# Paged attention: value pages issued from ScalarE, probabilities copied out ahead of the next maximum

## The reference

```python
def latent_attention(q_lat, q_rope, k_lat, k_rope, q_pos, k_pos):
    s = (jnp.einsum('bqhc,bkc->bhqk', ql, k_lat).astype(jnp.float32)
         + jnp.einsum('bqhr,bkr->bhqk', qr, k_rope).astype(jnp.float32)) * scale
    s = jnp.where(k_pos[None, :] <= qp[:, None], s, NEG_INF)
    p = jax.nn.softmax(s, axis=-1).astype(k_lat.dtype)
    return jnp.einsum('bhqk,bkc->bqhc', p, k_lat)
...
past = [(cache_ckv[j][page_table].reshape(bs, n_pages * PAGE_SIZE, MLA_KV_LORA),
         cache_krope[j][page_table].reshape(bs, n_pages * PAGE_SIZE, MLA_D_ROPE))
```

## Time and profile before

| | |
|---|---|
| median of 3 runs | 4748.0 us (4743.9 to 4748.29) |
| profiled execution | 4758.49 us, span 4756.7 us |
| TensorE busy | 4029.0 us, 85% |
| VectorE busy | 3155.6 us, 66% |
| ScalarE busy | 1374.6 us, 29% |
| GpSimd busy | 1164.6 us, 24% |
| mean granted TensorE clock | 0.931 |
| paged attention | from about 2728 us to 2995 us |

### The profile page before, as it was taken

One profiled execution on the slowest core, in us unless ns is written; L12 is line 12 of the kernel. 1 busy time (PEld: TensorE's weight loads), 2 busy tenths in 40 slices (PEclk: granted clock), 3 DMA queues, 4 the chain that ended last, 5 costly groups with the idle time before them and its releaser, 6 DMA issues.

```text
span 4756.7 us, 60298 instructions
## 1 busy us (share of the span) xinstructions
PE 4029.0 (85%) x19517; PEld 3147.9 (66%) x19517; DVE 3155.6 (66%) x6719; ACT 1374.6 (29%) x2253; POOL 1164.6 (24%) x1217
## 2 busy tenths in 40 slices
PE   8999678857999999999488868889569999999994
PEld 1454334456999999999346512344469999999994
DVE  0134556996878878878545512558977887887886
ACT  0120013366333333333112100123573333333331
POOL 0000011275323323323100000002672332333332
PEclk9998689989999999999779978899799999999997
DMA  9777675445888888887377666744458888888883
GB/s 317 248 259 248 230 244 196 158 171 221 293 288 284 292 285 285 291 287 259 142 241 228 195 185 198 233 163 161 173 220 270 284 292 285 285 291 287 284 288 118
DMA packets 494570, 1151.15 MB, mean 242 GB/s; under 512 B 45310, under 2 KB 268559, under 8 KB 491104
## 3 DMA queue, kind: packets, MB, share of 16 engines
q1 hardware_dynamic: 293330, 689.92, 42.9%
q0 software_dynamic: 95824, 350.11, 22.5%
q10 hardware_dynamic: 105296, 109.71, 6.7%
HBM read 952.47 MB, written 197.09 MB: 242 GB/s over the span
## 4 chain that ended last, share of the span: by engine, by line
PE 53%; DVE 19%; DMA 9%; ACT 7%; issue 6%; SPq 3%; POOL 2%; POOLq 1%; ACTq 0%; DVEq 0%
PE ps L1550 16%; PE ps L1531 12%; PE ps L1547 6%; PE ps L272 4%; DMA arena<-in_peer_uT 4%; PE ps L440 3%; ACT u_parts_d L1584 3%; DMA x<-in_peer_uT 3%; DVE v_parts_d L1688 2%; PE ps L251 2%; DVE u_parts_d L1684 2%; DVE arena L1722 2%; DVE x L1705 1%; ACT arena L1449 1%; DVE a_parts_d L1697 1%
## 5 line engine op out<-in xcount | busy, mean ns | idle before, releaser
L1531 PE MATMUL ps<-h_parts_d,u_parts_d 128*128 128x384 f32 x6144 | 1114.5, 337 | 114.1 <-DVE u_parts_d L1684 70.8
L1531 PEld LDWEIGHTS ps<-h_parts_d,u_parts_d 128*128 128x128 f32 x6144 | 1066.2, 188 | 153.3 <-ACT arena L1591 99.2
L1550 PE MATMUL ps<-a_parts_d,v_parts_d 128*128 128x384 f32 x4608 | 809.0, 334 | 0.0
L1550 PEld LDWEIGHTS ps<-a_parts_d,v_parts_d 128*128 128x128 f32 x4608 | 799.6, 188 | 0.0
L272 PE MATMUL ps<-ring,hT 128*128 128x512 f32 (+1 forms) x1440 | 645.5, 607 | 24.4 <-DMA ring<-in_gla_wo 13.7
L1586 ACT ACTIVATE v_parts_d<-ring 128x1024 fp32r<-128x1024 f32 x256 | 250.1, 1048 | 940.3 <-PE ps L1550 940.3
L272 PEld LDWEIGHTS ps<-ring,hT 128*128 128x128 f32 (+1 forms) x1440 | 253.4, 179 | 392.0 <-issue 387.7
L1684 DVE TENSOR_TENSOR u_parts_d<-ring,u_parts_d 128x1024 fp32r<-128x1024 f32 x256 | 313.5, 1225 | 198.0 <-ACT u_parts_d L1584 197.4
L1653 POOL DMA_INDIRECT arena<-in_peer_v,arena x256 | 243.3, 950 | 815.4 <-DVE ps L1722 806.7
L1653 POOL DMA_INDIRECT hT<-u_rows,arena x256 | 291.8, 1140 | 373.0 <-DVE hT L1705 329.2
L1722 DVE SCALAR_TENSOR_TENSOR ps<-arena,ps 128x1024 f32<-128x1024 f32 x256 | 329.3, 1286 | 16.2 <-DVE arena L1712 11.3
(11 more groups left out here) (277 smaller groups left out, 4487.9 us busy)
## 6 DMA issues: line engine op xcount, KB each, us to landing
ring<-in_peer_uT SPq DMA_DIRECT2D x256, 512.0 KB, 5.9
ring<-in_peer_v SPq DMA_DIRECT2D x256, 512.0 KB, 7.3
arena<-in_peer_uT SPq DMA_DIRECT2D x186, 512.0 KB, 5.5
u_rows<-arena SPq DMA_DIRECT2D x440, 128.0 KB, 4.0
ring<-in_ada_w SPq DMA_DIRECT2D x96, 512.0 KB, 4.6
gates_dense<-arena ACTq DMA_DIRECT2D x24, 2048.0 KB, 6.3
x<-gates_dense ACTq DMA_DIRECT2D x64, 768.0 KB, 7.8
u_rows<-arena SPq DMA_DIRECT2D x76, 512.0 KB, 6.0
```

Source lines behind the costliest of these rows:

```text
L1531: mm = e.matmul(ps[:, tt % 2, 0:ND], w[:, m], hR[:, v, k], start=(k == 0 and n == 0), stop=(k == KC - 1 and n == 2))
L1550: mm = e.matmul(ps[:, 4 + m % 2, 0:ND], w[:, rows], aR[:, v, tt], start=begins, stop=ends)
```

## The change

The loads of the value pages move from SyncE's function to ScalarE's. The per-page steps become a helper `pages` that both call. SyncE keeps the key pages with their wait for `s_ps`. ScalarE waits for the page table, issues the value pages of sequences 0 and 1, and then for each sequence computes its exponentials, waits for `s_ol` and issues the value pages of the sequence two further on; the exponentials of the last two stand behind the loop. On VectorE `probs_out` of the sequence before now stands ahead of `maximum`.

```diff
+            def pages(e, reg, i, u, buf, src, landed):
+
+                for q in range(NPAGE):
+                    e.reg_load(reg, table[0:1, bass.ds((i * 2 + u) * NPAGE + q, 1)])
+                    pg = e.snap(reg, min_val=0, max_val=src.shape[0] - 1)
+                    e.dma_start(buf[:, u, q], src[bass.ds(pg, 1)].rearrange("a p n -> (a p) n")).then_inc(landed, 16)
+
             def sp3(e):
...
                         for u in range(2):
-                            for buf, src, landed, freed in ((keys, d["page_keys"], keys_of[u], s_ps), (vals, d["page_values"], vals_of[u], s_ol)):
-
-                                e.wait_ge(freed, i * 2 + (u + 1))
-                                alone(e)
-                                for q in range(NPAGE):
-                                    e.reg_load(reg, table[0:1, bass.ds((i * 2 + u) * NPAGE + q, 1)])
-                                    pg = e.snap(reg, min_val=0, max_val=src.shape[0] - 1)
-                                    e.dma_start(buf[:, u, q], src[bass.ds(pg, 1)].rearrange("a p n -> (a p) n")).then_inc(landed, 16)
+                            e.wait_ge(s_ps, i * 2 + (u + 1))
+                            alone(e)
+                            pages(e, reg, i, u, keys, d["page_keys"], keys_of[u])
...
             def act3(e):
+                def exponentials(i, v):
+                    e.wait_ge(s_nmax, i * 2 + (v + 1))
+                    e.activation(pr[0:32, v, 0:PAST], ps[0:32, 0:4, :].rearrange("p b n -> p (b n)"), ACT.Exp, bias=sm[0:32, v, 1, 0:1],
+                                 scale=MSCALE, accum_out=sm[0:32, v, 2, 0:1])
+                    e.activation(pr[0:32, v, PAST:PAST + DEC_T], sm[0:32, v, 0, 0:DEC_T], ACT.Exp, bias=sm[0:32, v, 1, 0:1], scale=MSCALE,
+                                 accum_out=sm[0:32, v, 3, 0:1]).then_inc(s_exp, 1)
+
+                def values_in(i, v):
+                    e.wait_ge(s_ol, i * 2 + (v + 1))
+                    alone(e)
+                    pages(e, reg, i, v, vals, d["page_values"], vals_of[v])
+
                 e.sem_inc(s_exp, 1)
...
+                e.wait_ge(table_in, 16)
+                with e.register("value_page") as reg:
+                    values_in(0, 0)
+                    values_in(0, 1)
+                    with e.Fori(0, DEC_B // 2 - 1) as i:
+                        for v in range(2):
+                            exponentials(i, v)
+                            values_in(i + 1, v)
+                    exponentials(DEC_B // 2 - 1, 0)
+                    exponentials(DEC_B // 2 - 1, 1)
...
                 def front(i, u):
                     own_tokens(i, u)
-                    maximum(i, u)
                     if u:
                         probs_out(i, u - 1)
+                    maximum(i, u)
                     normalise(i, u)
```

More of the change, by code:

```diff
@@ L2247, in act3 @@
             def act3(e):
-                e.sem_inc(s_exp, 1)
[L2249 to L2256, removed]
+                def exponentials(i, v):
[8 more added lines that the diff above has]
+                    pages(e, reg, i, v, vals, d["page_values"], vals_of[v])
+                e.sem_inc(s_exp, 1)
+                e.wait_ge(table_in, 16)
[8 more added lines that the diff above has]
+                    exponentials(DEC_B // 2 - 1, 1)
             def dve3(e):
```

## The result

The changed kernel takes 4843.4 us (median of 4 runs, 4823.5 to 4856.9) against 4748.15 before: ratio 1.0197, 95% interval 1.0177 to 1.0217. It is slower by 95 us; 4820 was predicted, 72 slower. The profiled execution is the slowest of the four, 4856.9 us against 4758.5 of the profile before. Sequences are called lots, as in the prediction.

What follows compares the result with a forecast made beforehand. SyncE's page issuing was taken as the bound, 29.1 us a lot; the new serial chain summed to 42.0 us, run six times after a start 5.7 us earlier, adding 71.6 to 4748.0 for 4820 us, range 4780 to 4868.

Steps and rivals of the forecast that it cites:

- the ring: Paged attention: value end, ScalarE issues, exponentials, normalising, copies, scores and next values run in series, 42.0 us a lot against 29.1.
- Dear issuing: Rival: slow ScalarE register loads or queues hindering each other, 1.5 us a page, 4886 us; 6%.
- The rival in which the transfers are the limit: Paged attention: issues only seem to be the limit, so no change, 4748 us; 2%.
- The rival in which ScalarE's issues are as good as free: Exponentials not held up, so faster than before; with nothing held up, 4703 us; 4%.
- Cheap and dear issuing: Rivals on ScalarE's page cost: 0.45 us a page, 4785 us, 7%; or 1.5 us, 4886 us, 6%.
- V to exponential: End of a lot's values to the last of ScalarE's 16 value-page issues, ahead of the next exponentials: 13.6 us.
- exponential to scores: Exponentials and normalising, 4.0 us, then copy of values and own tokens until TensorE starts scores, 1.2 us.
- scores to transposes: TensorE's scores up to the transposes, after idle with a lowered clock: 13.5 us, upper bound 15.7.
- values: TensorE's value matmuls of a lot, behind a short idle: 7.6 us, against 9.3 behind a longer idle.
- V(0): End of the values of lot 0: forecast at 2796.6 us, 5.7 us before the old kernel's 2802.35.
- V(6): End of the values of lot 6: forecast at 3048.6 us against 2977.0, 71.6 us later.
- Part 2: VectorE copies the probabilities out ahead of the next maximum: 1.8 us less wait plus faster values, 3.5 us a lot.

Runs made afterwards that it cites:

- e3: Changed kernel with ScalarE issuing the value pages of b + 2 behind the exponentials of b + 1, not ahead of them: 4713.6 us, ratio 0.9922.
- e8: Changed kernel with value pages issued by GpSimd and only the exponentials on ScalarE: 4719.6 us, ratio 0.9911.
- e6: Changed kernel with ScalarE loading only 8 of the 16 value pages of each sequence: 4800.9 us, ratio 1.0082.
- e9: Changed kernel with 42 dummy matmuls filling TensorE's idle time behind the values of sequences 0 to 5: 4817.7 us, ratio 1.0145.
- e4: As e3, but VectorE keeps the old order, maximum ahead of the copy: 4740.4 us, ratio 0.9979.
- e2: Changed kernel with VectorE's old order of maximum and copy, so only the issues move to ScalarE: 4861.6 us, ratio 1.0234.
- e1: Kernel before with only VectorE's new copy order; SyncE still issues all pages: 4748.1 us, ratio 0.9997.
- e5: The changed kernel run again, nothing altered: 4846.8 us, ratio 1.0183.

## Why the prediction was right, and where it was short

The mechanism held at each step. The exponential starts 0.1 to 0.5 us behind the last of 16 issues; TensorE sits idle some 20 us ahead of the scores and 0.87 ahead of the values; DMA share is 0.41 in the stage (0.4 was forecast); outside the stage 3 us changed. The side was right for the reason given: e3 takes the order out of the ring and all the loss goes, with the same 128 issues in the same queue. Dear issuing, in either form (slow register loads on ScalarE, or queues that hinder each other), falls with it too. The rival in which the transfers are the limit falls with e3 and e8: steps of 24.1 and 23.8 us for the same bytes in 29.1 before. The rival in which ScalarE's issues are as good as free falls with e6: half of them are worth 6.2 us a lot. Cheap and dear issuing, at 0.45 and 1.5 us a page, stand on either side of the measured 0.91.

The forecast was 23 us short in the median and 27 in the profiled execution. By the terms of the ring, as the means of six turns in the profile after:

| term | predicted | measured | reason |
|---|---|---|---|
| V to exponential | 13.6 | 14.9 | 0.91 us a page on ScalarE |
| exponential to scores | 5.2 | 5.1 | |
| scores to transposes | 13.5 | 14.6 | clock, 12.9 to 16.0 |
| transposes to values | 2.1 | 2.1 | |
| values | 7.6 | 8.2 | clock, 7.6 or 9.3 |
| sum | 42.0 | 44.9 | |

Two terms were mis-sized. The first is the page on ScalarE. I took SyncE's 12.53 us for 16 value pages and added 30 ns a page for the issue instruction alone. The rows of the profile after for the line of the register load, to set beside the earlier trace rows, and ScalarE's 32 issues at the start of the stage:

```profile
L2184 ACTq TENSOR_LOAD <-arena x128: 282/287/481, 2729.5 to 3036.7; - x128
...
L2184 SPq TENSOR_LOAD <-arena x128: 261/268/470, 2729.7 to 2983.6; - x128
L2184 ACTq FUSED_REGOPS  x96: 46/46/66, 2800.4 to 3036.6; - x96
...
2730.14 26.53 ACTq L2186 DMA_DIRECT2D arena<-in_page_values  x32
```

And of the kernel before, where all 128 of these instructions belong to key pages:

```profile
L2194 SPq FUSED_REGOPS  x128: 52/52/66, 2729.9 to 2945.1; - x128
```

14.0 us for 16, the mean of six, is (14.0 - 0.34) / 15 = 0.91 a page, against (12.53 - 0.33) / 15 = 0.81. Of these 100 ns the load makes up 19 and the issue 11 (344 against 333). The rest goes with a register step (FUSED_REGOPS) ahead of the load. On SyncE before, each key page had it and no value page: the key pages cost (14.15 - 0.33) / 15 = 0.92. On ScalarE the 96 value pages of the loop have it, and the 32 at the start, which do not, cost (26.53 - 0.34) / 31 = 0.85. So ScalarE is hardly dearer than SyncE for the same steps (0.91 against 0.92 with the step, 0.85 against 0.81 without), and the row to go by was the other one of the earlier trace rows. With 0.1 us more ahead of the first issue and 0.25 behind the last, the term is 1.3 us a lot short, 8 us in all.

The second is the clock. I took the scores at 13.5, from one stretch behind 14.2 us of idle in the profile before, and kept 15.7 for the upper bound only. That profile had three more lots with over 3 us of idle ahead of their scores. Here are lots 3 and 7; lot 5 took 13.51 behind 3.73 us:

```profile
2832.86 14.55 PE L2211 MATMUL ps<-arena 128*32 128x512 f32 x24 [3.47 <-DMA arena<-in_page_keys]
...
2948.49 15.45 PE L2211 MATMUL ps<-arena 128*32 128x512 f32 x24 [3.48 <-DMA arena<-in_page_keys]
```

Up to the transposes lots 1, 3, 5 and 7 took 14.5 us on average, and 14.6 was measured after. The term was one row taken out of a spread; idle of 20 us cost no more here than idle of 3.5. Five of the eight lots after had their 24 score matmuls in 15.4 to 15.7 us, the other three in 12.7 to 13.3. Two stretches of the profile after:

```profile
2820.00:2833.00 13.00, 12.91 (x30) 2.46 (x30) 0.00 (x0) 0.00 (x0) 0.00 (x0) 0.89 0.00 1
2906.20:2921.70 15.50, 15.49 (x25) 2.37 (x25) 0.00 (x0) 0.00 (x0) 0.00 (x0) 0.72 0.00 0
```

Both begin behind 19.8 us of idle of TensorE; one was granted 0.89, the other 0.72. The values were taken at 7.6 because the wait ahead of them would be 0.87 us; the wait was 0.87 in all eight lots, but four of them took 9.3. Together the two make 1.7 us a lot, 10 us in all, and 6 at the start: scores of lots 0 and 1 at 15.5 and 15.6, values of lot 0 at 9.3. For the scores e9 shows it to be the clock that falls in the idle time: with that time filled, five of six take 11.29 at a granted 1.00.

The start itself was mis-sized the other way. I held 305 GB/s for the full rate; 26 us of the profile after moved 340:

```profile
2731.00:2757.00 26.00, 7.61 (x9) 1.25 (x10) 0.70 (x5) 0.00 (x0) 0.00 (x0) 0.50 1.02 340
```

So the first keys lost 2.0 us to the values (19.0 from the first issue to the scores, against 17.0 in the earlier trace rows) and not 4.1, and the scores of lot 0 began at 2749.4, not 2751.7. V(0) is at 2800.3, 3.7 late: 6 of clock less 2.3 of this. 3.7 and 6 x 2.9 make the 21 us by which V(6) is late, 3070.0 against 3048.6; 5 to 6 more lie behind it (values of lot 7 at 9.3, the output projection, the start of the next stages at a low clock). The profiled execution was also the slowest of its four.

Part 2 came out at 3.0 us a lot (e4 against e3) and 2.8 (e2 against the changed kernel) where 3.5 were forecast, and at nothing while SyncE binds (e1). The 1.8 us of wait is as argued; the faster values came in full only in e1.

The Trainium skill says that issuing from several engines saves only the sequencer's time, and that this is usually small beside the transfer (DMA: Bandwidth & Descriptors, section "Issuing engines are not separate DMA queues"). For these pages it is not small: a value page costs its queue 0.81 us or more, where 128 KB at the 340 GB/s seen above are 0.39 us, and e3 and e8 save 5 us a lot with the same bytes. The Trainium skill also says that ScalarE's queue is strict FIFO (TensorE: Matmul & The Clock Gate, section "Architectural detail: the array is 16× 32×32, not 1× 128×128"). The trace agrees: an exponential whose maximum was ready at 2793.8 started at 2814.97, behind a wait and 16 issues that it has nothing to do with.

## What to carry to other kernels

Before loads are moved to a computing engine's queue, write down what stands behind their wait on that queue and when it is wanted: here the same 128 issues cost 95 us in one place of ScalarE's program and gain 37 in the next. A wait for a buffer to come free belongs behind the work that the consumer's engine needs next, or on an engine with nothing behind it, even if each issue is dearer there. Price an issue by a row with the same register steps, not only the same transfer. Where a change adds idle time ahead of matmuls, take the mean of all the trace's rows with idle ahead of them, and not the nearest row: here that would have given 14.5 us for the scores, with 14.6 measured.

## What the runs showed of the hardware

- A page load with its address from a register costs 0.81 us of queue on SyncE, and 0.85 on ScalarE, for 128 KB. With one more register step ahead of the load it is 0.91 on ScalarE and 1.00 on GpSimd, and 0.92 on SyncE for 192 KB.
- Two queues with loads of 128 and 192 KB moved 340 GB/s over 26 us, where SyncE alone, held by its issuing, moved 180 between 2747 and 2987.
- The same 24 score matmuls took 11.3 us behind 1.4 us of idle, 13.5 to 15.5 behind 3.5 to 3.7 us (before), and 12.7 to 15.7 behind 20 us (after), without a pattern that the rows explain; with the idle filled, 11.3 in five of six. In the first four runs of the changed kernel the time goes with the granted clock, in the four of e5 it does not. Why the clock comes back sooner in one turn than in the next is open.
